# Eight split weight tiles in place of six, a 1 KB DMA scratch and another order of work at stage ends

## The reference

```python
for i in range(2):                               # layers of the first block
    mod = cond @ ada_w[i] + ada_b[i]             # 1024 x 6144: shift, scale, gate (twice)
    h = rmsnorm(x, norm1_g[i]) * (1 + scale1) + shift1
    y = diff_attention(h, ...) if i == 0 else axial_gqa(h, ...)
    x = x + gate1 * y
    h = rmsnorm(x, norm2_g[i]) * (1 + scale2) + shift2
    x = x + gate2 * ((silu(h @ w_gate) * (h @ w_up)) @ w_out)
x = rmsnorm(x, final_g)
proj = rms_norm(x, mix_norm_g) @ w_in            # the second block
y_a = u * (tril(w_spatial) @ rms_norm(v) + b)    # 4 groups of 128 x 128, on gelu of a part of proj
y_b = dilated_mixture_attention(q, k, v)
x = x + (gates_0 * (y_a @ w_branch_a) + gates_1 * (y_b @ w_branch_b)) @ w_out
a, val = split(rms_norm(x, ffn_norm_g) @ w_up)
x = x + (gelu(causal_conv(a)) * val) @ w_down
return rms_norm(x, final_norm_g)
```

## Time and profile before

| | |
|---|---|
| median of 3 runs | 1038.43 us |
| lowest and highest run | 1037.96 and 1038.45 us |
| profiled execution, first to last instruction (its span) | 1033.8 us |
| mean granted TensorE clock | 0.992 |
| PE busy | 986.3 us (95%) |
| DVE busy | 740.2 us (72%) |
| ACT busy | 542.6 us (52%) |
| POOL busy | 68.4 us (7%) |
| read from HBM | 217.96 MB, 212 GB/s over the span |

### The profile page before, as it was taken

The page is one execution under the profiler, slowest core; times in us unless marked ns, Lnnn a source line. Parts: engine busy times, 40 slices in busy tenths (PEclk is TensorE's granted clock), DMA queues, the critical chain, the costliest instruction groups (busy, mean ns, idle before and its releaser), DMA issues.

```text
span 1033.8 us, 13550 instructions
## 1 busy us (share of the span) xinstructions
PE 986.3 (95%) x5102; PEld 827.2 (80%) x5102; DVE 740.2 (72%) x1053; ACT 542.6 (52%) x875; POOL 68.4 (7%) x126
## 2 busy tenths in 40 slices
PE   2999799999999999999999999999999999999997
PEld 2887577888878787778888886888888779999986
DVE  5988888878877897887665447647753777777643
ACT  4466846544443485575444436575546474444442
POOL 2100222000000411010000002000000010000000
PEclk8999999999999999999999999999999999999999
DMA  9998167998889472449865553856444367656551
GB/s 339 371 371 285 39 204 230 344 321 295 273 304 359 162 250 101 143 127 321 263 203 186 183 184 108 269 160 205 134 142 143 119 190 218 187 177 189 184 184 41
DMA packets 126968, 219.89 MB, mean 213 GB/s; under 512 B 9235, under 2 KB 78088, under 8 KB 126904
## 3 DMA queue, kind: packets, MB, share of 16 engines
q1 hardware_dynamic: 125200, 215.52, 63.4%
q0 software_dynamic: 1088, 2.87, 0.8%
q10 hardware_dynamic: 616, 0.65, 0.2%
HBM read 217.96 MB, written 1.05 MB: 212 GB/s over the span
## 4 chain that ended last, share of the span: by engine, by line
PE 84%; DVE 8%; ACT 4%; issue 2%; DMA 1%; POOL 0%; SPq 0%; POOLq 0%; DVEq 0%; ACTq 0%
PE bank L1900 13%; PE bank L1902 13%; PE bank L1901 13%; PE bank L1913 5%; PE bank L1915 5%; PE bank L1914 5%; PE bank L2504 3%; PE bank L2505 3%; PE bank L2506 3%; DVE w_lo L1156 2%; PE bank L1961 2%; PE bank L1963 2%; PE bank L1962 2%; ACT w_hi L638 1%; DVE ada_acc L1186 1%
## 5 line engine op out<-in xcount | busy, mean ns | idle before, releaser
L1156 DVE TENSOR_TENSOR w_lo<-raw,w_hi 128x1024 fp32r<-128x1024 f32 x312 | 379.1, 1223 | 215.3 <-ACT w_hi L638 214.5
L638 ACT ACTIVATE w_hi<-raw 128x1024 fp32r<-128x1024 f32 x312 | 328.2, 1061 | 338.4 <-PE bank L1902 139.7
L1900 PE MATMUL bank<-w_hi,h_hi 128*128 128x512 f32 x608 | 244.3, 402 | 3.7 <-DVE w_lo L1156 3.7
L1902 PE MATMUL bank<-w_hi,h_lo 128*128 128x512 f32 x608 | 238.3, 392 | 0.0
L1901 PE MATMUL bank<-w_lo,h_hi 128*128 128x512 f32 x608 | 237.9, 391 | 0.0
L1900 PEld LDWEIGHTS bank<-w_hi,h_hi 128*128 128x128 f32 x608 | 114.8, 189 | 28.4 <-issue 6.1
L1902 PEld LDWEIGHTS bank<-w_hi,h_lo 128*128 128x128 f32 x608 | 114.7, 189 | 24.6
L1901 PEld LDWEIGHTS bank<-w_lo,h_hi 128*128 128x128 f32 x608 | 114.9, 189 | 23.6 <-issue 1.0
L2504 PE MATMUL bank<-h_hi,w_hi 128*128 128x256 f32 x320 | 90.8, 284 | 1.1 <-DVE conv_t L1828 1.1
L2505 PE MATMUL bank<-h_hi,w_lo 128*128 128x256 f32 x320 | 90.7, 283 | 0.0
L2506 PE MATMUL bank<-h_lo,w_hi 128*128 128x256 f32 x320 | 90.7, 283 | 0.0
(11 more groups left out here) (328 smaller groups left out, 1372.2 us busy)
## 6 DMA issues: line engine op xcount, KB each, us to landing
raw<-in_f_w_in SPq DMA_DIRECT2D x176, 256.0 KB
ada<-in_ada_w SPq DMA_DIRECT2D x86, 512.0 KB, 5.9
raw<-in_w_in SPq DMA_DIRECT2D x46, 512.0 KB
raw<-in_f_w_out SPq DMA_DIRECT2D x44, 512.0 KB
raw<-in_w_up SPq DMA_DIRECT2D x88, 256.0 KB
raw<-in_a_w_qkv SPq DMA_DIRECT2D x24, 512.0 KB
raw<-in_w_down SPq DMA_DIRECT2D x22, 512.0 KB
raw<-in_b_w_qkv SPq DMA_DIRECT2D x12, 512.0 KB
```

The lines of the kernel that those rows point to most:

```text
L638: nc.scalar.activation(w_hi[:, m % SPL], raw[:, m % RAW], ACT.Copy).then_inc(hi_done, 1)
L1156: ve.tensor_tensor(w_lo[:, m % SPL], raw[:, m % RAW], w_hi[:, m % SPL].bitcast(F32), ALU.subtract).then_inc(lo_done, 1)
L1900: mm(o, hi, w_hi[:, s, k], start=(u == 0 and k == 0), stop=False)
L1902: last = mm(o, lo, w_hi[:, s, k], start=False, stop=(u == 3 and k == 1))
```

## The change

- `SPL` is 8. The places in the programs keep their expression `BASE + SPL + j`, so ACT's splits and DVE's lows at a given place are of tiles two further on. The tables go by tile number, so that folds and their loads come two tiles of PE's work earlier; `TAKE_AFTER` moves one entry from 99 to 101.
- At the start ACT's `for m in range(1, SPL + AHEAD)` makes splits 1 to 9, where it made 1 to 7, before `h_hi` of the second half, and DVE makes lows 5 to 8, where it made 5 and 6, before `modulate(1)`; `fold(16)` goes with `low(8)`.
- At stage ends the operand's second piece goes before the last residual, the first split and low go behind the scaling of the second half, and the last two stand together.
- Memory for the larger rings comes from POOL's DMA scratch (1 KB where the default is 16 KB), from `w_spT`, from one `SIDE` buffer less, and from `w_spatial`, which is now loaded late, after the last fold, into the freed `ada` buffers; it is transposed at tile 12 of IN_C and copied at tile 15.

The diff, without the semaphores' names and numbers and without two lines in the loader that change nothing for the tiles here:

```diff
@@ -36,7 +36,8 @@
-SPL = 6
+SPL = 8
+SCRATCH = 1024
@@ -51,6 +52,8 @@
+ADA_END = 96
+SP_TURN, SP_TAKE = 12, 15
@@ -68,7 +71,7 @@
-TAKE_AFTER = {68: 6, 81: 7, 99: 9}
+TAKE_AFTER = {68: 6, 81: 7, 101: 9}
@@ -225,7 +227,7 @@
-        w_sp = at_p("w_sp", [P, 4, P], 9216)
+        w_sp, w_spT = (ada[:, 0, a].rearrange("p (g s) -> p g s", g=4) for a in range(2))
@@ -545,19 +549,12 @@
             norm(0)
-            pool.wait_ge(ada_done, 8)
-            pool.dma_start(w_sp[:], w_spatial[0].rearrange("g t s -> t g s")).then_inc(side_in, 16)
             lanes = same_lane[:].rearrange("p a n -> p (a n)")
 ...
                                         pattern=[[-1, P]], channel_multiplier=1).then_inc(lane_ok, 1)
-
-            pool.wait_ge(side_in, 16)
-
-            nc.gpsimd.affine_select(out=w_sp[:], in_=w_sp[:], compare_op=ALU.is_ge, fill=0.0, base=0,
-                                    pattern=[[0, 4], [-1, P]], channel_multiplier=1).then_inc(setup_p, 1)
             pool.wait_ge(ada_done, 12)
@@ -607,6 +604,11 @@
+            pool.wait_ge(ada_done, ADA_END)
+            pool.dma_start(w_sp, w_spatial[0].rearrange("g t s -> t g s")).then_inc(sp_in, 16)
+            pool.wait_ge(sp_in, 16)
+            nc.gpsimd.affine_select(out=w_sp, in_=w_sp, compare_op=ALU.is_ge, fill=0.0, base=0,
+                                    pattern=[[0, 4], [-1, P]], channel_multiplier=1).then_inc(sp_low, 1)
@@ -710,18 +712,18 @@
                 part_operand(o, 0, 1, gain, shift)
+                part_square(r, 1, 0)
+                part_operand(o, 0, 2, gain, shift)
+                part_square(r, 1, 1)
+                part_operand(o, 0, 3, gain, shift)
+                part_scale(r, 1)
                 split(first)
-                part_square(r, 1, 0)
-                part_square(r, 1, 1)
-                part_operand(o, 0, 2, gain, shift)
-                part_operand(o, 0, 3, gain, shift)
-                split(first + 1)
-                part_scale(r, 1)
                 for p in range(2):
                     part_operand(o, 1, p, gain, shift)
-                split(first + 2)
+                split(first + 1)
                 part_operand(o, 1, 2, gain, shift)
                 part_operand(o, 1, 3, gain, shift)
+                split(first + 2)
                 split(first + 3)
@@ -813,9 +815,6 @@
                     split(QKV_A + SPL + m)
-                if m == 8:
-                    act.wait_ge(setup_t, 3)
-                    nc.scalar.activation(w_spT[:], bank[7][:].rearrange("p (g t) -> p g t", g=4), ACT.Copy).then_inc(setup, 1)
                 if m == 9:
@@ -991,6 +990,9 @@
+                    if 8 * turn + j == SP_TAKE:
+                        act.wait_ge(sp_t, 1)
+                        nc.scalar.activation(w_spT, bank[7][:].rearrange("p (g t) -> p g t", g=4), ACT.Copy).then_inc(sp_ok, 1)
@@ -1305,18 +1307,18 @@
                 part_operand(o, 0, 0, gain, shift)
+                part_operand(o, 0, 1, gain, shift)
                 part_residual(r, s, nxt, 1, 1, gated)
-                part_operand(o, 0, 1, gain, shift)
-                low(first)
                 part_operand(o, 0, 2, gain, shift)
                 part_operand(o, 0, 3, gain, shift)
-                low(first + 1)
                 part_scale(r, 1)
+                low(first)
                 for p in range(2):
                     part_operand(o, 1, p, gain, shift)
-                low(first + 2)
+                low(first + 1)
                 part_operand(o, 1, 2, gain, shift)
                 part_operand(o, 1, 3, gain, shift)
+                low(first + 2)
                 low(first + 3)
@@ -1361,8 +1363,8 @@
                 fold(a)
-            low(5)
-            low(SPL)
+            for m in range(5, SPL + 1):
+                low(m)
             modulate(1)
@@ -1503,8 +1505,8 @@
                 make_gains(N2_V, 4)
-                low(IN_0)
-                low(IN_0 + 1)
+                low(WO_A + 2 + SPL)
+                low(WO_A + 3 + SPL)
@@ -2058,11 +2060,6 @@
                     reduce_vector(1)
-                if m == 7:
-                    pe.wait_ge(setup_p, 1)
-                    for g in range(4):
-                        last = nc.tensor.transpose(bank[7][:, g * P:(g + 1) * P], w_sp[:, g], ident[:])
-                    last.then_inc(setup_t, 1)
@@ -2336,6 +2333,11 @@
+                if m == SP_TURN:
+                    pe.wait_ge(sp_low, 1)
+                    for g in range(4):
+                        last = nc.tensor.transpose(bank[7][:, g * P:(g + 1) * P], w_sp[:, g], ident[:])
+                    last.then_inc(sp_t, 1)
@@ -2350,6 +2352,7 @@
+                pe.wait_ge(sp_ok, 1)
@@ -2555,7 +2558,7 @@
-    nc = bacc.Bacc("TRN2", target_bir_lowering=False, num_devices=1)
+    nc = bacc.Bacc("TRN2", target_bir_lowering=False, num_devices=1, dynamic_dma_scratch_size=SCRATCH)
```

More of the change, by code:

```diff
@@ L26 @@
 EPS = 1e-6
-SIDE = 8
+SIDE = 7
 VECS = 11
@@ L169, in program @@
         rope_c_sb = sb("rope_c_sb", [P, T, 2, 16])
-        w_spT = sb("w_spT", [P, 4, P])
         REG_U = 2 * KF * S * 4
@@ L273, in program @@
         setup_t = sem("setup_t")
-        setup_p = sem("setup_p")
+        sp_in, sp_low, sp_t, sp_ok = sem("sp_in"), sem("sp_low"), sem("sp_t"), sem("sp_ok")
         dve = sem("dve")
@@ L352, in load_wide @@
                 slot_free(m, turn)
+                m = at(m, turn, LOOP)
                 src = w.rearrange("(k p) n -> p k n", p=P)[:, 2 * u:2 * u + 2, cols(c0, turn, per, n)]
@@ L1376, in minus_lambda_end @@
             def minus_lambda_end():
-                v_.wait_ge(setup, 4)
+                v_.wait_ge(setup, 3)
                 link(ve.tensor_tensor(neg_lam, stat[:, MISC + 5:MISC + 6], stat[:, MISC + 4:MISC + 5], ALU.subtract))
@@ L1402, in angles @@
                 ve.tensor_copy(stat[:, MISC + 7:MISC + 8], stat[:, MISC + 2:MISC + 3]).then_inc(setup_v, 1)
-                v_.wait_ge(setup, 5)
+                v_.wait_ge(setup, 4)
                 for h in range(2):
```

## The result

| | before | changed |
|---|---|---|
| median of the runs | 1038.20 us (4 runs) | 1055.76 us (4 runs, 1055.36 to 1057.71) |
| ratio, 95% interval | | 1.0166 (1.0149 to 1.0184) |
| profiled execution, its span | 1033.8 us | 1056.0 us |
| time of the profiled execution | | 1057.71 us |
| granted TensorE clock | 0.992 | 0.986 |

The change makes the kernel slower by 17.6 us. The forecast was 1047.4 (1040 to 1053): the sign was right, the time lies outside.

A forecast was written before the change was run, and what follows sets the result against it. PE's work plus its waits bound the kernel; start 5.0, attention 2.5, stage ends 1.3 and small terms 0.3 add 9.1 us to the 1033.8 us span, with 4.6 around it 1047.5, stated as 1047.4 us, range 1040 to 1053.

The forecast's parts named there:

- The start: Before PE's tile 6: splits, lows and fold 16 now ahead of `mod` delay `h_lo`, with `low(8)` awaiting tile 8's landing; +5.0 us.
- rival (c): Clock falls once or twice more, at the start's stall or the wait at 142 us; +1.7 us each, 1049.1 to 1050.8; chance 0.15.
- Attention A: Two more folds at its beginning +1.4 us, two more before the last `att` +2.0, `mod`'s wait gone −0.9; together +2.5.
- Stage ends: At r = 0 to 4, shorter waits for `h_lo` but later last lows; together +1.3 us, from −4 to +5.
- rival (a): Faster: waits at stage ends go, the tails cost nothing; below 1036.3 us, or 1033.7 if every such wait vanishes; chance 0.12.
- The small terms: FF0's end +0.5 us, `block_sums` −0.8, attention B +0.6, late `w_spatial` 0, POOL's scratch 0; together +0.3.
- The clock: The dip after 149 to 153 us may go, the stall at 46 us may bring one; netted to 0.
- rival d: The 1 KB scratch makes POOL's DMAs wait for descriptors; decides only above 3.8 us each; 1052 us at 4.5; chance 0.05.
- The signs: Trace observations, at tile 6, attention and stage ends, named beforehand as showing the forecast right or wrong.
- right: Tile 6 waits 4.6 to 5.4 us; stage-end `h_lo` waits fall to about 0.2 each, `act_u` waits grow about 1.
- wrong: Tile 6 is not waited for, waits for `act_u` shrink, or PE waits somewhere for a tile's load.

The follow-up runs named there:

- e2: The changed kernel (eight tiles) with the old order of work in boundary at stage ends: 1046.93 us, 1.0075.
- e4: The changed kernel with each feed-forward stage's first silu and product, and the last block's first copy, behind the same tile as with six: 1050.07 us, 1.0109.
- e12: The changed kernel with splits and lows back in place at stage ends, only DVE's second operand piece ahead of the residual: 1047.20 us, 1.0085.
- e3: The changed kernel with the first operand's second half back ahead of splits 8 and 9, lows 7 and 8 and fold 16: 1057.48 us, 1.0164.
- e16: Changed kernel with six tiles, eight raw buffers, old stage-end order but for the piece; late spatial matrix and 1 KB scratch kept: 1035.18 us, 0.9959.
- e11: The changed kernel (eight tiles) with old stage-end order but for the piece, and start, first steps of stages and folds put back: 1040.67 us, 1.0023.
- e7: The kernel before (six tiles) with only the new order of work in boundary, on ACT and DVE: 1077.59 us, 1.0363.

## Why the prediction was wrong

- **The start** cost +5.0 as said, but in this execution by another path, and that the sum came out is luck: 3.7 of wait in place of 5.0, and 1.3 net of half clock, which I had only as rival (c). And `low(8)` was not what decided here: tile 8 landed by 43.84, not 45.7, DVE took `mod` at 47.58, and then ACT's `h_hi` waited for split 9, which I had called no hindrance:

```profile
43.84 1.06 ACT L640 ACTIVATE w_hi<-raw 128x1024 fp32r<-128x1024 f32 x1 [2.88 <-DMA raw<-in_a_w_qkv]
47.89 1.06 ACT L640 ACTIVATE w_hi<-raw 128x1024 fp32r<-128x1024 f32 x1 [3.00 <-DMA raw<-in_a_w_qkv]
48.85 2.06 ACT L772 ACTIVATE h_hi<-hf,mod,gains 128x256 fp32r<-128x256 f32 x4
```

  In the profiled executions of e2 and e4, whose start is the same program, it went as the prediction has it: split 8 began on its landing at 45.37 and 44.86 us (45.7 said), ACT's `h_hi` then waited for DVE's `gains`, and PE waited 4.5 and 5.0 us. In e12 it went as here, with 3.0 us. So the chain was right, and which of the two landings decides changes from one execution to the next. e3 adds that undoing this wait gives nothing: the sum missed the debt behind it.
- **Attention A**: +2.5 said, about +1.8 measured up to the stage end. Entry +1.7 for 1.4; end +1.2 and half clock for 2.0; `mod`'s wait gone as said, and with it the old dip at 153 us.
- **Stage ends** is the step that failed: +1.3 said, about +14 measured (the rows of the list for r = 0 to 4). I wrote that "the last low ends later by about one low", and put +0.9 on each of r = 0, 2, 4. The gain in front came (−1.1, −1.7, −1.1). At r = 2 the term itself was near: the last low ended 1.4 us later. At r = 0 and r = 4 what was missed is that the step PE waits for stands behind a split *two tiles further on*, and that this split waits for a landing: I counted engines' instructions in that stretch, and not the loads, although the change moves every load's release. PE's next step came later by 3.0 us at r = 0 and 6.4 at r = 4, from landings, and by 2.2 at r = 2, mostly from the late low. The half clock at each cost 2.8, 1.9 and 1.6 more, and the sum had none. "Tiles are split two further ahead" stood in the prediction as a relief.
- **A row was misread** in the same step. The 1.6 us for `act_u` "in two places" are waits of L1925 at 294.90 and 574.84 us, which is where the two feed-forward stages *end*. Behind r = 0 PE did not wait in the kernel before (182.98 us); only r = 2 had such a wait (0.83 us). So "in the stages whose next steps on DVE or ACT PE already waits for" held for one of the two, and rival (a) counted 1.6 us that the stage ends have no part in.
- **The small terms** came out near: FF0's end +0.5, `block_sums` −1.0, attention B +1.0 for 0.6. POOL's `root` of the second half took 0.30 us in each of the stage ends r = 0, 1, 2 and 4 (172.00, 370.43, 457.74, 853.06), as good as the best I had allowed.
- **The clock** I netted to zero; it was +1.7 (1.3 after what came back), +1.3, +2.8, +1.6 and +1.9, against which only the old dip at 153 us went. Rival (c) was right as a mechanism and needed a longer list of waits.
- **The scratch** (rival d) does make POOL wait, see below, at no cost in time here.
- **The signs**: the waits for `h_lo` fell and those for `act_u` grew, as said for "right", but by 2.9 and 2.0 us where I had said 1. PE's wait at tile 6 was 3.3 us where I had said 4.6 to 5.4. "PE waits somewhere for a tile's load" stood under "wrong", and by way of ACT's splits it did.
- **No rival had the interaction**: the order alone +38 us, the rings alone +7.5, both +17.6.

## What to carry to other kernels

A deeper look-ahead in a program that an engine works through in order is also a *later* place for every other step in that program: each stands behind the input of a tile further on. When you enlarge a ring, keep the other steps behind the tile they stood behind, and ask of each first step of a stage which landing stands ahead of it. More buffers in front of the loads (raw) were worth more here than more behind them (split): the same memory gave −0.4% in the one place (e16) and +0.75% in the other (e2), or +0.2% with the other steps put back (e11). And before costing a stage end, ask which instruction in it frees a load's buffer.

## What the hardware showed that I had not expected

With 1 KB of scratch, the last of POOL's seven small DMAs at the start waited 7.5 us with nothing named as releaser. All fourteen kernels with 1 KB show this wait, of 4.9 to 7.5 us; the three with the default scratch don't, and the DMA followed at once (38.85 behind 38.13 in e7). The changed kernel:

```profile
38.52 0.74 POOL L562 DMA_DIRECT2D pos_i<-in_positions  x1
46.76 0.73 POOL L563 DMA_DIRECT2D rope_a_sb<-in_rope_a  x1 [7.50 <-issue]
```

The table landed 6.7 us after its issue and was first used at 68.7 us, so the wait cost nothing. Why it is the seventh, and what it waits for, no run here shows.

The half clock around a wait need not begin with the work. At the start it came after it: PE stood 3.3 us until 51.19; its matmuls started every 0.23 us until 52.68, and then every 0.43. The windows show the fall one window after the idle one (at r = 4, above, it was the other way round, and the clock was down before PE resumed):

```profile
46.00:51.00 5.00, 1.84 (x9) 1.16 (x7) 3.20 (x7) 3.02 (x5) 0.73 (x1) 1.00 1.00 363
51.00:56.00 5.00, 4.81 (x14) 3.90 (x15) 4.96 (x8) 2.12 (x2) 0.00 (x0) 0.67 0.95 327
```

POOL's seven selections on `same_lane` took 7.41 us here (from 13.67) where they took 2.90 in e7 (from 20.59). Here they ran beside DVE's folds (5.45 us from 14.19); there DVE was idle for the most part. The Trainium skill ("SBUF — State Buffer", section "SBUF: two separate sides") has a DVE instruction with two inputs in SBUF and a GpSimd instruction that reads SBUF exclude each other; the trace agrees, with 7.41 against 2.90 us. Between all kernels it is 6.5 to 7.6 us for the fourteen that have them beside the folds and 2.9 to 3.2 us for the three that don't.
